# ConvGLU feed-forward of a hybrid decoder block: one 512-column product for both token parts

## The chip, the core and the metric

The kernel runs on one core of one Trainium2 chip. The metric is the device time of one launch in microseconds (us). TensorE (PE in the rows, PEld for its weight loads), VectorE (DVE), ScalarE (ACT), GpSimd (POOL) and the DMA queues work side by side and wait for one another by semaphores.

## The reference, cut to what matters

One decoder block on 256 tokens of width 1024: a mixing part with three branches (attention, a state-space scan, cross-attention to 256 memory tokens), merged and projected, and then a convolutional feed-forward part. The change works in the feed-forward part:

```python
def causal_dwconv(x, w, b):            # width 3, per channel
    ...
# in hybrid_layer:
    hid = causal_dwconv(rms_norm(h, ffn_norm_g) @ w_ffn_up, ffn_conv_w, ffn_conv_b)
    g_ff, up = jnp.split(hid, 2, axis=-1)
    return h + (jax.nn.silu(g_ff) * up) @ w_ffn_down
```

`w_ffn_up` is 1024 x 5632 (2816 gate columns and 2816 up columns), `w_ffn_down` is 2816 x 1024. All is float32.

## The kernel before

**Products in three parts.** A float32 operand is split into a high part that TensorE takes in one pass and a low part, the rest. Instead of a*b the kernel sums high*high, high*low and low*high (`three`, L364 to L366). Tokens stand as `tok_hi` and `tok_lo` (8 tiles of 128 x 256, features on partitions), weights as `w_hi` and `w_lo`.

**Weights** come in chunks of 128 x 2048 elements (1 MB) through three slots, 0 to 2. SyncE issues the load once the slot's raw tile has been used up (`lo_ready`), ScalarE makes `w_hi` by a copy (`split_hi`, L332, once TensorE has finished with the slot's last chunk: `gemm_done`), VectorE makes `w_lo` by a subtraction (`split_lo`, L336, `lo_ready`), and TensorE may then use the chunk. A slot thus holds one chunk at a time, and a round number `r` counts its chunks.

**The feed-forward part** has 11 steps (`F_STEPS`) of 256 hidden columns. Step f has a gate chunk (slot 0), an up chunk (slot 1) and a chunk of `w_ffn_down` (slot 2). TensorE's order is gate(f), up(f), down of step f - 1 (`ffn_step`); it is a hardware loop for f = 2 to 8, and the last two steps are written out. The gate chunk's result (two column tiles of 256 tokens) fills PSUM bank 0, the up chunk's bank 1; `down` adds into banks 4 to 7. At the end of the part come, in this order: gate(9), up(9), gate(10) from slot 2, up(10) from slot 0, down of step 8 from slot 1, down of step 9 from slot 2 and, in five pieces (`down_end`), down of step 10 from slot 0.

**VectorE's step** (`ffn` at L1698, `pad_with` at L1700) is a fixed order: `pad_g` = bank times the tokens' norm factor `rstd_b` (L1702), `split_lo` of the down chunk, four tap operations of the gate convolution (L1715), `pad_u` (L1702), `silu_g` (L1723), `split_lo` of the *next* step's gate chunk, four taps for up, `hid` (L1729), `split_lo` of the next up chunk, `hid_lo` (L1733). In the last step (10) the `split_lo` behind `silu_g` is that of the chunk for down of step 9.

**ScalarE's step** (`ffn` at L1238): it begins the gate convolution (L1246, two operations, waits for `pad_g` by `bank_free`), `split_hi` of the next gate chunk, `tanh_g` (L1253, waits for the taps), begins the up convolution (L1246), `split_hi` of the next up chunk, `hid_hi` (L1257), `split_hi` of the next down chunk.

Each engine does its instructions in the order written. TensorE's wait ahead of gate(f+1) is for `lo_ready[0]`, that is the `split_lo` behind `silu_g` in step f.

Of the kernel before, what the change touches and what calls it, by code (L numbers as in the profile page):

```python
# [104 lines left out]
def build(nc, x, mem, w_in, b_gate, w_mem_kv, w_br_attn, w_br_ssm, w_br_mem, w_out, w_ffn_up, w_ffn_down,  # L105
# [4 lines left out]
    def place(name, at, shape, dtype=F32):  # L110
        return nc.alloc_sbuf_tensor_at(name, [P, *shape], dtype, offset=base + int(at * KB))
# [5 lines left out]

    tok_hi = place("tok_hi", 72, [KT, T], F32R)
    tok_lo = place("tok_lo", 80, [KT, T], F32R)

# [231 lines left out]
    def cols_part(pe, s, j, ks, o, hi, lo, k0=0, start=True, stop=True, tiles=None, **kw):  # L352
# [99 lines left out]
    with nc.Block() as block:  # L452
# [128 lines left out]
        def _(pe):  # L581
# [311 lines left out]
            for s in (1, 2):  # L893
                pe.wait_ge(lo_ready[s], RF + 3)
                pe.wait_ge(bank_free[s], RF + 2)
                open_bank(pe, s)
                for j in range(2):
                    cols_part(pe, s, j, range(0, HK), ps[:, s, j * T:(j + 1) * T], tok_hi, tok_lo, start=False,
                              stop=False, skip_group_check=True)
                if s == 1:  # L900
                    pe.wait_ge(h_added, 3)
                    turn_h(2)
                    turn_h(3)
                    pe.wait_ge(h_rstd, NT)
# [3 lines left out]
                    mm.then_inc(h_spread, 1)  # L908
            pe.wait_ge(h_lo, KT)
# [13 lines left out]
            def ffn_step(f, first=False):  # L923
# [3 lines left out]
                down(r, 2, f, hid_hi, hid_lo, first)  # L927

            ffn_step(1, first=True)
            with pe.Fori(2, F_STEPS - 2) as f:  # L930
                ffn_step(f)
            gemm_cols(pe, RL - 1, 0, tok_hi, tok_lo)
            gemm_cols(pe, RL - 1, 1, tok_hi, tok_lo)
            pe.wait_ge(bank_free[2], RF + 3)
            gemm_cols(pe, RL - 1, 2, tok_hi, tok_lo, free=())
            gemm_cols(pe, RL, 0, tok_hi, tok_lo)
            down(RL, 1, F_STEPS - 2, hid_hi, hid_lo)
# [8 lines left out]
        def _(act):  # L946
# [320 lines left out]
            ffn(F_STEPS - 1, 2, RF + 4, 0, RL + 2, [(RL, 2)], [(RL + 1, 0)], [], hi=end_hi)  # L1267
            for n, (t, c0, width, _) in enumerate(Y_PARTS):
# [17 lines left out]
        def _(dve):  # L1286
# [193 lines left out]
            def heads(i, first=False):  # L1480
# [36 lines left out]
                if i == 1:  # L1517
                    dve.wait_ge(m_factor_in, 16)
# [178 lines left out]

            def ffn(f, sa, ra, sb, rb, early, after_gate, after_up, hi=hid_hi, lo=hid_lo):  # L1698
# [161 lines left out]
```

## Time and profile before

| | us |
|---|---|
| median of 3 runs | 684.38 (683.76 to 684.55) |
| the profiled execution | 683.92 |
| its span, first to last instruction | 682.1 |
| TensorE busy | 673.5 |
| VectorE busy | 493.5 |
| ScalarE busy | 371.5 |
| one feed-forward step, from one `pad_g` to the next | 16.98 |

Outside the span lie 683.92 - 682.1 = 1.8 us. A busy TensorE is not yet a TensorE at its peak: products overlap, so the distance from one start to the next is what one of them costs, and the duration shown (0.28 us for 256 columns) is how long it takes until its result is there. On the other engines, too, the next instruction may start a little before the one ahead is shown as ended.

### The profile page before, as it was taken

What the parts mean: (1) busy time and instruction counts of PE and PEld (TensorE: products, weight loads), DVE (VectorE), ACT (ScalarE), POOL (GpSimd) and SP (SyncE); (2) the same over time, 40 slices, a digit from 0 to 9 for tenths busy, and PEclk for the clock granted to TensorE, in tenths of its full rate; (3) what the DMA queues carried; (4) which work ended last, traced back from release to release, by engine and by line L of the source; (5) the groups of instructions that cost most, each with busy time, mean ns of one, the idle gap of its engine ahead of it and who ended that gap; (6) DMA issues with size and microseconds to landing.
All of it is one profiled execution on the core that took longest, in us unless ns stands there. A gap on an engine that the chain in (4) does not pass through costs nothing.

```text
span 682.1 us, 11417 instructions
## 1 busy us (share of the span) xinstructions
PE 673.5 (99%) x4505; PEld 616.4 (90%) x4505; DVE 493.5 (72%) x617; ACT 371.5 (54%) x462; POOL 10.4 (2%) x21
## 2 busy tenths in 40 slices
PE   8999999999999999999999999999999999999996
PEld 6999999999999989999888888888899999999995
DVE  6886979696866766777754655556688777777796
ACT  7568767767455544555533333443555555555552
POOL 0000000000100000000000000000100000000001
PEclk9999999999999999999999999999999999999999
DMA  9775868569185446545566655565445555555521
GB/s 297 240 256 181 247 198 263 164 217 326 62 270 171 145 163 232 180 140 171 178 211 218 214 194 182 195 231 173 166 140 191 188 185 190 180 189 183 193 87 62
DMA packets 99599, 130.92 MB, mean 192 GB/s; under 512 B 5615, under 2 KB 73708, under 8 KB 98924
## 3 DMA queue, kind: packets, MB, share of 16 engines
q1 hardware_dynamic: 98020, 125.27, 55.8%
q10 hardware_dynamic: 1544, 5.16, 2.3%
q8 instruction: 25, 0.41, 0.3%
q14 instruction: 10, 0.08, 0.0%
HBM read 129.31 MB, written 2.68 MB: 193 GB/s over the span
## 4 chain that ended last, share of the span: by engine, by line
PE 97%; DVE 1%; DMA 1%; ACT 0%; POOL 0%; issue 0%; POOLq 0%; SPq 0%; DVEq 0%; ACTq 0%
PE ps L364 31%; PE ps L365 30%; PE ps L366 30%; PE ps L678 1%; DMA x_nat<-x 1%; PE ps L679 1%; PE ps L419 1%; PE ps L663 1%; PE ps L698 1%; PE ps L715 1%; PE ps L706 0%; DVE h_nat L1750 0%; PE ps L697 0%; PE ps L717 0%; PE ps L771 0%; PE ps L666 0%
## 5 line engine op out<-in xcount | busy, mean ns | idle before, releaser
L336 DVE TENSOR_TENSOR w_lo<-w_raw,w_hi 128x2048 fp32r<-128x2048 f32 x107 | 244.6, 2287 | 88.0 <-ACT w_hi L332 88.0
L332 ACT ACTIVATE w_hi<-w_raw 128x2048 fp32r<-128x2048 f32 x107 | 204.3, 1911 | 99.1 <-PE ps L366 93.9
L364 PE MATMUL ps<-tok_hi,w_hi 128*128 128x256 f32 x864 | 246.6, 285 | 0.4 <-DVE tok_lo L1310 0.4
L365 PE MATMUL ps<-tok_lo,w_hi 128*128 128x256 f32 x864 | 244.4, 283 | 0.0
L366 PE MATMUL ps<-tok_hi,w_lo 128*128 128x256 f32 x864 | 244.4, 283 | 0.0
L364 PEld LDWEIGHTS ps<-tok_hi,w_hi 128*128 128x128 f32 x864 | 165.7, 192 | 2.0 <-issue 1.5
L365 PEld LDWEIGHTS ps<-tok_lo,w_hi 128*128 128x128 f32 x864 | 165.7, 192 | 0.4
L366 PEld LDWEIGHTS ps<-tok_hi,w_lo 128*128 128x128 f32 x864 | 165.7, 192 | 0.0
L364 PE MATMUL ps<-w_hi,tok_hi 128*128 128x512 f32 x128 | 50.2, 392 | 0.0
L365 PE MATMUL ps<-w_lo,tok_hi 128*128 128x512 f32 x128 | 49.9, 390 | 0.0
L366 PE MATMUL ps<-w_hi,tok_lo 128*128 128x512 f32 x128 | 49.8, 389 | 0.0
L1246 ACT ACTIVATE conv_g<-pad_g,params 128x256 f32<-128x256 f32 x22 | 12.1, 595 | 38.5 <-DVE pad_g L1702 38.5
L1395 DVE SCALAR_TENSOR_TENSOR conv_a<-pad_x,params,conv_a 128x256 f32<-128x256 f32 x72 | 29.5, 478 | 0.2
L366 PEld LDWEIGHTS ps<-w_hi,tok_lo 128*128 128x128 f32 x128 | 24.0, 188 | 5.1
L364 PEld LDWEIGHTS ps<-w_hi,tok_hi 128*128 128x128 f32 x128 | 24.1, 188 | 4.9 <-issue 0.2
L365 PEld LDWEIGHTS ps<-w_lo,tok_hi 128*128 128x128 f32 x128 | 24.0, 188 | 4.7
L364 PE MATMUL ps<-w_hi,hid_hi 128*128 128x512 f32 x72 | 28.1, 391 | 0.0
L365 PE MATMUL ps<-w_lo,hid_hi 128*128 128x512 f32 x72 | 28.1, 391 | 0.0
L366 PE MATMUL ps<-w_hi,hid_lo 128*128 128x512 f32 x72 | 28.0, 389 | 0.0
L364 PE MATMUL ps<-w_hi,os_hi 128*128 128x512 f32 x64 | 25.1, 392 | 0.0
L365 PE MATMUL ps<-w_lo,os_hi 128*128 128x512 f32 x64 | 24.9, 390 | 0.0
L366 PE MATMUL ps<-w_hi,os_lo 128*128 128x512 f32 x64 | 24.9, 389 | 0.0
(269 smaller groups left out, 1002.2 us busy)
## 6 DMA issues: line engine op xcount, KB each, us to landing
w_raw<-w_in SPq DMA_DIRECT2D x94, 512.0 KB, 4.8
w_raw<-w_ffn_up SPq DMA_DIRECT2D x44, 512.0 KB, 4.4
w_raw<-w_ffn_down SPq DMA_DIRECT2D x22, 512.0 KB, 4.1
w_raw<-w_mem_kv SPq DMA_DIRECT2D x16, 512.0 KB, 4.4
w_raw<-w_br_ssm SPq DMA_DIRECT2D x16, 512.0 KB, 4.9
acs_b<-acs_d ACTq DMA_DIRECT2D x4, 1024.0 KB, 6.3
w_raw<-w_br_attn SPq DMA_DIRECT2D x8, 512.0 KB, 4.8
w_raw<-w_br_mem SPq DMA_DIRECT2D x8, 512.0 KB, 4.6
```

The lines of the kernel that those rows point to most:

```text
L332: act.activation(w_hi[:, s, :], w_raw[:, s, :], ACT.Copy).then_inc(hi_ready[s], 1)
L336: dve.tensor_tensor(w_lo[:, s, :], w_raw[:, s, :], w_hi[:, s, :].bitcast(F32), ALU.subtract).then_inc(lo_ready[s], 1)
L364: pe.matmul(o, a[0], b[0], start=start, stop=False, **kw)
L365: pe.matmul(o, a[0], b[1], start=False, stop=False, **kw)
L366: return pe.matmul(o, a[1], b[0], start=False, stop=stop, **kw)
L419: return pe.transpose(ps[:, bank, o:o + P], src[:, t, k * P:(k + 1) * P], ident)
L663: mm = pe.transpose(ps[:, 3 + t, c * P:(c + 1) * P], conv_o[:, 2 + c, t * P:(t + 1) * P], ident)
L678: pe.matmul(o, x_dt[:, 0, h * SHD:(h + 1) * SHD], decay[:, h, 0:T], start=True, stop=False)
L679: mm = pe.matmul(o[:, P:T], x_dt[:, 1, h * SHD:(h + 1) * SHD], decay[:, h, T:T + P], start=False, stop=True)
L698: mm = pe.matmul(ps[:, 3 + a, P:3 * P], q_t[:, a, P:T], k_t[:, a, :], start=True, stop=True)
L1246: act.activation(conv[:, j, :], pad[:, j, FTAPS - 1:], ACT.Identity, bias=cols_up[:, FTAPS, bass.ds(c, 1)], scale=cols_up[:, FTAPS - 1, ba ...
L1395: dve.scalar_tensor_tensor(conv_a[:, s, j, :], pad_x[:, s, j, tap:tap + T], cols_conv[:, tap, bass.ds(conv_tile(s, j, g), 1)], conv_a[:, s ...
```

## The change

From step 2 on (`wide=True`) a gate or up chunk is multiplied otherwise. The two token parts now lie side by side in one tile `tok` (8 x 2 x 256), and one product of 512 columns of `w_hi` with both parts writes a whole PSUM bank: high*high in its left half, high*low in its right half. The third product (`w_lo` with the high part, 256 columns) adds to the left half. So a chunk's column tile fills a bank of its own, and a chunk fills two: banks 0 and 1 for gate, 2 and 3 for up. The sum of the halves is then made outside TensorE. ScalarE copies the right halves of both banks to `low_g` or `low_u`, VectorE adds the left halves to it (this frees the banks, `bank_free`), and multiplies by `rstd_b` in a second operation (`pad_scaled`). Steps 0 and 1, and all products ahead of the feed-forward part, are as they were. Some semaphores are merged: `m_factor_kept` and `m_factor_in` are one, and `h_spread` counts on `late_turned`, with the counts waited for set to match.

```diff
-    tok_hi = place("tok_hi", 72, [KT, T], F32R)
-    tok_lo = place("tok_lo", 80, [KT, T], F32R)
+    tok = place("tok", 72, [KT, 2, T], F32R)
+    tok_hi, tok_lo = tok[:, :, 0, :], tok[:, :, 1, :]
...
+    def gemm_both(pe, s, banks, both, other=None):
+        for j in range(2):
...
+            for k in range(KT):
+                w = slice(k * CW + j * P, k * CW + (j + 1) * P)
+                pe.matmul(ps[:, banks[j], :], w_hi[:, s, w], both[:, k], start=k == 0, stop=False)
+                mm = pe.matmul(ps[:, banks[j], 0:T], w_lo[:, s, w], both[:, k, 0, :], start=False, stop=k == KT - 1)
+        mm.then_inc(gemm_done[s], 1)
...
+            def wide_steps(r):
+                for s in range(2):
+                    pe.wait_ge(lo_ready[s], r + 2)
+                    pe.wait_ge(bank_free[s], r + 1)
+                    gemm_both(pe, s, F_BANKS[s], tok)
...
             with pe.Fori(2, F_STEPS - 2) as f:
-                ffn_step(f)
+                r = f + (RG - 1)
+                wide_steps(r)
+                down(r, 2, f, hid_hi, hid_lo)
+            wide_steps(RL - 1)
+            pe.wait_ge(lo_ready[2], RL + 1)
+            pe.wait_ge(bank_free[0], RL + 1)
+            gemm_both(pe, 2, F_BANKS[0], tok)
+            pe.wait_ge(lo_ready[0], RL + 2)
+            pe.wait_ge(bank_free[1], RL + 1)
+            gemm_both(pe, 0, F_BANKS[1], tok)
```

In ScalarE's `ffn`:

```diff
-                    act.wait_ge(bank_free[s], freed)
+                    if wide:
+                        act.wait_ge(gemm_done[s], freed - 1)
+                        act.activation(low[:], part_pair(F_BANKS[n], 1), ACT.Copy).then_inc(low_part, 1)
+                        act.wait_ge(pad_scaled, 2 * f + n - 3)
+                    else:
+                        act.wait_ge(bank_free[s], freed)
```

In VectorE's `pad_with`:

```diff
-                    dve.wait_ge(gemm_done[s], r + 1)
-                    dve.tensor_tensor(pad[:, :, FTAPS - 1:], halves(s), rstd_b[:].unsqueeze(1).to_broadcast([P, 2, T]),
-                                      ALU.mult).then_inc(bank_free[s], 1)
+                    if wide:
+                        n = int(pad is pad_u)
+                        dve.wait_ge(low_part, LOW0 + 2 * f + n - 3)
+                        dve.tensor_tensor(pad[:, :, FTAPS - 1:], part_pair(F_BANKS[n], 0), (low_g, low_u)[n][:],
+                                          ALU.add).then_inc(bank_free[s], 1)
+                        dve.wait_ge(bank_free[s], RF + 4 if s > 1 else r + 2)
+                        dve.tensor_tensor(pad[:, :, FTAPS - 1:], pad[:, :, FTAPS - 1:], rstd,
+                                          ALU.mult).then_inc(pad_scaled, 1)
```

ScalarE in step 9, the first that is written out (the loop's steps are in the same order). Before:

```order
L1246 ACTIVATE conv_g<-pad_g,params 128x256 [waits g_silu,bank_free0]
L1246 ACTIVATE conv_g<-pad_g,params 128x256
L332 ACTIVATE w_hi<-w_raw 128x2048 [waits gemm_done0,loaded0]
L1253 ACTIVATE tanh_g<-conv_g 128x512 [waits f_step]
L1246 ACTIVATE conv_u<-pad_u,params 128x256 [waits hid_done,bank_free1]
L1246 ACTIVATE conv_u<-pad_u,params 128x256
```

and now:

```order
L1277 ACTIVATE low_g<-ps 128x512 [waits gemm_done0]
L1285 ACTIVATE conv_g<-pad_g,params 128x256 [waits g_silu,pad_scaled]
L1285 ACTIVATE conv_g<-pad_g,params 128x256
L337 ACTIVATE w_hi<-w_raw 128x2048 [waits gemm_done0,loaded0]
L1292 ACTIVATE tanh_g<-conv_g 128x512 [waits f_step]
L1277 ACTIVATE low_u<-ps 128x512 [waits gemm_done1]
L1285 ACTIVATE conv_u<-pad_u,params 128x256 [waits hid_done,pad_scaled]
L1285 ACTIVATE conv_u<-pad_u,params 128x256
```

A copy out of PSUM stands ahead of each convolution's begin; that of the up chunk stands behind `tanh_g`, which waits for the taps (`f_step`).

VectorE in step 9 and, in its last rows, at the start of what follows. Before:

```order
L1702 TENSOR_TENSOR pad_g<-ps,rstd_b 128x2x256 [waits gemm_done0]
L336 TENSOR_TENSOR w_lo<-w_raw,w_hi 128x2048 [waits hi_ready2]
L1715 SCALAR_TENSOR_TENSOR conv_g<-pad_g,params,conv_g 128x256 [waits conv_begun] x2
L1715 SCALAR_TENSOR_TENSOR conv_g<-pad_g,params,conv_g 128x256 [waits f_step] x2
L1702 TENSOR_TENSOR pad_u<-ps,rstd_b 128x2x256 [waits gemm_done1]
L1723 SCALAR_TENSOR_TENSOR silu_g<-tanh_g,conv_g 128x512 [waits g_tanh]
L336 TENSOR_TENSOR w_lo<-w_raw,w_hi 128x2048 [waits hi_ready0]
```

and now:

```order
L1744 TENSOR_TENSOR pad_g<-ps,low_g 128x2x256 [waits low_part]
L1747 TENSOR_TENSOR pad_g<-pad_g,rstd_b 128x2x256 [waits bank_free0]
L341 TENSOR_TENSOR w_lo<-w_raw,w_hi 128x2048 [waits hi_ready2]
L1763 SCALAR_TENSOR_TENSOR conv_g<-pad_g,params,conv_g 128x256 [waits conv_begun] x2
L1763 SCALAR_TENSOR_TENSOR conv_g<-pad_g,params,conv_g 128x256 [waits f_step] x2
L1744 TENSOR_TENSOR pad_u<-ps,low_u 128x2x256 [waits low_part]
L1747 TENSOR_TENSOR pad_u<-pad_u,rstd_b 128x2x256 [waits bank_free1]
L1771 SCALAR_TENSOR_TENSOR silu_g<-tanh_g,conv_g 128x512 [waits g_tanh]
L341 TENSOR_TENSOR w_lo<-w_raw,w_hi 128x2048 [waits hi_ready0]
```

Each `pad_g` and `pad_u` is two operations, the first of which waits for ScalarE's copy (`low_part`) and no longer for TensorE; the last row is the `split_lo` of the chunk for up(10); in the loop it stands for the next step's gate chunk.

VectorE in step 10, from `last_lo` of step 9 to the `split_lo` of the chunk that down of step 9 uses (slot 2). Before:

```order
L1733 TENSOR_TENSOR last_lo<-hid,last_hi 128x512 [waits hid_hi_s]
L1702 TENSOR_TENSOR pad_g<-ps,rstd_b 128x2x256 [waits gemm_done2]
L1715 SCALAR_TENSOR_TENSOR conv_g<-pad_g,params,conv_g 128x256 [waits conv_begun] x2
L1715 SCALAR_TENSOR_TENSOR conv_g<-pad_g,params,conv_g 128x256 [waits f_step] x2
L1702 TENSOR_TENSOR pad_u<-ps,rstd_b 128x2x256 [waits gemm_done0]
L1723 SCALAR_TENSOR_TENSOR silu_g<-tanh_g,conv_g 128x512 [waits g_tanh]
L336 TENSOR_TENSOR w_lo<-w_raw,w_hi 128x2048 [waits hi_ready2]
```

and now:

```order
L1781 TENSOR_TENSOR last_lo<-hid,last_hi 128x512 [waits hid_hi_s]
L1744 TENSOR_TENSOR pad_g<-ps,low_g 128x2x256 [waits low_part]
L1747 TENSOR_TENSOR pad_g<-pad_g,rstd_b 128x2x256 [waits bank_free2]
L1763 SCALAR_TENSOR_TENSOR conv_g<-pad_g,params,conv_g 128x256 [waits conv_begun] x2
L1763 SCALAR_TENSOR_TENSOR conv_g<-pad_g,params,conv_g 128x256 [waits f_step] x2
L1744 TENSOR_TENSOR pad_u<-ps,low_u 128x2x256 [waits low_part]
L1747 TENSOR_TENSOR pad_u<-pad_u,rstd_b 128x2x256 [waits bank_free0]
L1771 SCALAR_TENSOR_TENSOR silu_g<-tanh_g,conv_g 128x512 [waits g_tanh]
L341 TENSOR_TENSOR w_lo<-w_raw,w_hi 128x2048 [waits hi_ready2]
```

Nothing of TensorE's work lies between these rows; both pads, the taps and `silu_g` stand ahead of that `split_lo`, and the pads are two operations each.

## Rows read from the trace of the kernel before

**Rows 1.** The page, part 1: busy time of each engine

```profile
PE 673.5 (99%) x4505; PEld 616.4 (90%) x4505; DVE 493.5 (72%) x617; ACT 371.5 (54%) x462; POOL 10.4 (2%) x21
```

**Rows 2.** The page, part 4: the chain that ended last, by engine

```profile
PE 97%; DVE 1%; DMA 1%; ACT 0%; POOL 0%; issue 0%; POOLq 0%; SPq 0%; DVEq 0%; ACTq 0%
```

**Rows 3.** Groups by line, 460 to 682 us: busy, mean ns | idle before, releaser

```profile
L1666 DVE TENSOR_TENSOR h_nat<-ps,h_nat 128x512 f32<-128x512 f32 x4 | 2.8, 689 | 3.2 <-PE ps L366 3.2
...
L1196 ACT ACTIVATE mg_hi<-ps 128x512 fp32r<-128x512 f32 x2 | 1.1, 596 | 3.9 <-PE ps L419 3.9
```

**Rows 4.** Timeline of TensorE, a loop step: start, us, what, [idle before]

```profile
562.85 0.40 PE L364 MATMUL ps<-w_hi,hid_hi 128*128 128x512 f32 x1
...
568.09 0.39 PE L366 MATMUL ps<-w_hi,hid_lo 128*128 128x512 f32 x1
568.32 0.28 PE L364 MATMUL ps<-tok_hi,w_hi 128*128 128x256 f32 x1
...
573.95 0.28 PE L366 MATMUL ps<-tok_hi,w_lo 128*128 128x256 f32 x1
```

**Rows 5.** Timeline of VectorE over one loop step

```profile
574.27 0.69 DVE L1702 TENSOR_TENSOR pad_g<-ps,rstd_b 128x512 f32<-128x512 f32 x1 [2.62 <-PE ps L366]
574.88 2.28 DVE L336 TENSOR_TENSOR w_lo<-w_raw,w_hi 128x2048 fp32r<-128x2048 f32 x1
577.08 1.66 DVE L1715 SCALAR_TENSOR_TENSOR conv_g<-pad_g,params,conv_g 128x256 f32<-128x256 f32 x4
580.03 0.69 DVE L1702 TENSOR_TENSOR pad_u<-ps,rstd_b 128x512 f32<-128x512 f32 x1 [1.29 <-PE ps L366]
580.64 0.68 DVE L1723 SCALAR_TENSOR_TENSOR silu_g<-tanh_g,conv_g 128x512 f32<-128x512 f32 x1
581.24 2.28 DVE L336 TENSOR_TENSOR w_lo<-w_raw,w_hi 128x2048 fp32r<-128x2048 f32 x1
583.44 1.66 DVE L1715 SCALAR_TENSOR_TENSOR conv_u<-pad_u,params,conv_u 128x256 f32<-128x256 f32 x4
...
591.25 0.69 DVE L1702 TENSOR_TENSOR pad_g<-ps,rstd_b 128x512 f32<-128x512 f32 x1 [2.62 <-PE ps L366]
```

**Rows 6.** Timeline of ScalarE in the same step

```profile
575.20 1.10 ACT L1246 ACTIVATE conv_g<-pad_g,params 128x256 f32<-128x256 f32 x2 [3.88 <-DVE pad_g L1702]
...
578.78 0.63 ACT L1253 ACTIVATE tanh_g<-conv_g 128x512 f32<-128x512 f32 x1 [0.67 <-DVE conv_g L1715]
...
585.87 0.63 ACT L1257 ACTIVATE hid_hi<-hid 128x512 fp32r<-128x512 f32 x1 [2.06 <-DVE hid L1729]
586.40 1.90 ACT L332 ACTIVATE w_hi<-w_raw 128x2048 fp32r<-128x2048 f32 x1
```

**Rows 7.** Timeline of VectorE, steps 9 (first row) and 10

```profile
642.19 0.69 DVE L1702 TENSOR_TENSOR pad_g<-ps,rstd_b 128x512 f32<-128x512 f32 x1 [2.62 <-PE ps L366]
...
656.55 0.68 DVE L1702 TENSOR_TENSOR pad_g<-ps,rstd_b 128x512 f32<-128x512 f32 x1
657.90 1.77 DVE L1715 SCALAR_TENSOR_TENSOR conv_g<-pad_g,params,conv_g 128x256 f32<-128x256 f32 x4 [0.67 <-ACT conv_g L1246]
...
661.32 2.29 DVE L336 TENSOR_TENSOR w_lo<-w_raw,w_hi 128x2048 fp32r<-128x2048 f32 x1
```

**Rows 8.** Timeline of ScalarE, step 10: `tanh_g`

```profile
660.07 0.61 ACT L1253 ACTIVATE tanh_g<-conv_g 128x512 f32<-128x512 f32 x1
```

**Rows 9.** Timeline of TensorE, the first product of down of step 9

```profile
664.74 0.39 PE L364 MATMUL ps<-w_hi,last_hi 128*128 128x512 f32 x1
```

**Rows 10.** Timeline of VectorE, then TensorE, near 9 us: a start after a wait

```profile
9.06 0.48 DVE L1310 SCALAR_TENSOR_TENSOR tok_lo<-ps,cols_mix,tok_hi 128x256 fp32r<-128x256 f32 x1 [0.48 <-ACT tok_hi L964]
...
9.70 0.35 PE L364 MATMUL ps<-tok_hi,w_hi 128*128 128x256 f32 x1 [0.45 <-DVE tok_lo L1310]
9.89 0.28 PE L365 MATMUL ps<-tok_lo,w_hi 128*128 128x256 f32 x1
```

**Rows 11.** Timeline of TensorE, its first products, before anything else runs

```profile
0.98 4.59 PE L413 MATMUL ps<-zero_s 128*128 128x512 bf16 x13 [0.98 <-DVE zero_s L1287]
```

More of the change, by code:

```diff
@@ L60 @@
 SLOTS = 3
+LOW0 = 0
 Q = 32
@@ L65 @@
 HK = KT // 2
+F_BANKS = (0, 1), (2, 3)
 V_BANKS, G1_BANKS, OUT_BANKS, H_BANKS = (2, 5), (0, 7), ((2, 3), (6, 7)), (4, 5, 0, 3)
@@ L225, in build @@
     silu_g = place("silu_g", R + 10.5, [2, T])
+    low_g = place("low_g", R + 24, [2, T])
+    low_u = place("low_u", R + 26, [2, T])
     hid = place("hid", R + 12.5, [2, T])
@@ L360, in cols_part @@
         return mm
+    def gemm_both(pe, s, banks, both, other=None):
+        for j in range(2):
+            if other is not None and j:
+                pe.wait_ge(*other)
+            for k in range(KT):
[3 more added lines that the diff above has]
+        mm.then_inc(gemm_done[s], 1)
     def three(pe, o, a, b, start, stop, **kw):
@@ L927, in ffn_step @@
                 down(r, 2, f, hid_hi, hid_lo, first)
+            def wide_steps(r):
[3 more added lines that the diff above has]
+                    gemm_both(pe, s, F_BANKS[s], tok)
             ffn_step(1, first=True)
+            pe.wait_ge(bank_free[1], RG + 2)
+            pe.wait_ge(bank_free[2], RF + 3)
             with pe.Fori(2, F_STEPS - 2) as f:
-                ffn_step(f)
[L932 to L936, printed above, removed]
+                r = f + (RG - 1)
[8 more added lines that the diff above has]
+            gemm_both(pe, 0, F_BANKS[1], tok)
             down(RL, 1, F_STEPS - 2, hid_hi, hid_lo)
@@ L1235, in _, with ffn @@
             split_hi(act, RG, 0)
-            def ffn(f, sa, na, sb, nb, after_gate, after_up, last, first=False, hi=hid_hi):
-                for n, (s, freed, pad, conv, tile) in enumerate(((sa, na, pad_g, conv_g, 0),
-                                                                 (sb, nb, pad_u, conv_u, FT))):
-                    act.wait_ge(bank_free[s], freed)
+            def ffn(f, sa, na, sb, nb, after_gate, after_up, last, first=False, hi=hid_hi, wide=True):
+                for n, (s, freed, pad, conv, tile, low) in enumerate(((sa, na, pad_g, conv_g, 0, low_g),
+                                                                      (sb, nb, pad_u, conv_u, FT, low_u))):
+                    if wide:
[4 more added lines that the diff above has]
+                        act.wait_ge(bank_free[s], freed)
                     if not first:
@@ L1259, in ffn @@
                     split_hi(act, rr, ss)
-            ffn(0, 1, RF + 3, 2, RF + 3, [(RG, 1)], [(RG, 2)], [(RG + 1, 0)], first=True)
-            ffn(1, 0, RG + 2, 1, RG + 2, [], [(RG + 1, 1)], [(RG + 1, 2)])
+            ffn(0, 1, RF + 3, 2, RF + 3, [(RG, 1)], [(RG, 2)], [(RG + 1, 0)], first=True, wide=False)
+            ffn(1, 0, RG + 2, 1, RG + 2, [], [(RG + 1, 1)], [(RG + 1, 2)], wide=False)
             with act.Fori(2, F_STEPS - 2) as f:
@@ L1695, in _, with ffn @@
             dve.wait_ge(pads_zero, 2)
-            def ffn(f, sa, ra, sb, rb, early, after_gate, after_up, hi=hid_hi, lo=hid_lo):
+            def ffn(f, sa, ra, sb, rb, early, after_gate, after_up, hi=hid_hi, lo=hid_lo, wide=True):
                 def pad_with(s, r, pad, splits):
-                    dve.wait_ge(gemm_done[s], r + 1)
-                    dve.tensor_tensor(pad[:, :, FTAPS - 1:], halves(s), rstd_b[:].unsqueeze(1).to_broadcast([P, 2, T]),
-                                      ALU.mult).then_inc(bank_free[s], 1)
+                    rstd = rstd_b[:].unsqueeze(1).to_broadcast([P, 2, T])
+                    if wide:
[6 more added lines that the diff above has]
+                                          ALU.mult).then_inc(pad_scaled, 1)
+                    else:
+                        dve.wait_ge(gemm_done[s], r + 1)
+                        dve.tensor_tensor(pad[:, :, FTAPS - 1:], halves(s), rstd, ALU.mult).then_inc(bank_free[s], 1)
                     for rr, ss in splits:
```

29 lines of the change are left out of this document (16 added, 13 removed).

## The prediction, made before the kernel had run

> **What bounds the kernel now.** I read the page's first part and its chain first. TensorE is busy for 673.5 of 682.1 us [rows 1], and the chain that ended last is 97% TensorE [rows 2]. So the time is that of TensorE's stream, and only two things count: how many microseconds of products the change takes out, and whether the stream begins to wait. For the second I read the timelines of one step. The step is 591.25 - 574.27 = 16.98 us [rows 5]. VectorE waits in it twice for TensorE, 2.62 us ahead of `pad_g` and 1.29 us ahead of `pad_u` [rows 5]: 3.91 us of slack in all. That is what the change spends from.
>
> **What TensorE saves.** What a product costs is the distance between starts. 24 products of 512 columns stand from 562.85 to 568.32, 0.228 each (0.227 without the first), and 48 of 256 columns from 568.32 on, the last at 573.95: 5.63 / 47 = 0.120 [rows 4]. Before, a pair high*high and high*low with its third product costs 3 x 0.120 = 0.360; now 0.227 + 0.120 = 0.347. A chunk has 16 such sets: 5.76 us before, 5.55 now. Nine steps have 18 chunks: 288 x 0.013 = 3.7 us is the most that can be won, and one step of TensorE becomes 2 x 5.55 + 24 x 0.227 = 16.55 us. The product count falls by a third and the gain is small, since columns are what costs: 512 and 256 columns at 2.4 GHz take 0.213 and 0.107, so each product has 0.013 to 0.014 us beside its columns.
>
> The Trainium skill, "TensorE: Matmul & The Clock Gate", section "Back-to-back issue gap", gives N / 2.4 + 2.5 ns. The trace does not agree, with 13 ns. By the page's figure a chunk would be (estimate) 16 x 0.0025 = 0.04 us shorter instead of 0.21, and the sum below some 1.4 us higher.
>
> **What VectorE and ScalarE get.** VectorE gets one operation of 512 elements more for each pad: `pad_g` takes 0.69 and the next starts 0.61 after it [rows 5]. An add of PSUM and an SBUF tile takes the same 0.689 [rows 3]. But the multiply waits for the add by a semaphore, so it starts at its end: 0.69 + 0.03 = 0.72 (0.61 is the lower bound). ScalarE gets a copy of 512 elements out of PSUM, 0.596 by `mg_hi` [rows 3]; the nearest from SBUF, `hid_hi`, is 0.63 [rows 6]. In sums of busy time it all fits (VectorE 16.98 - 3.91 + 2 x 0.72 = 14.5 of 16.55). It is the order that matters. `low_u` stands behind `tanh_g`, and `tanh_g` waits for VectorE's taps; so VectorE stands still from the taps' end until `tanh_g` and the copy are through, and behind the stopped `pad_u` are queued `silu_g` and the `split_lo` that TensorE's next gate chunk waits for.
>
> **The chain of a loop step**, from the end of gate(f)'s last product as zero (before: 573.95 + 0.28 = 574.24, and `pad_g` started 0.03 later [rows 4, 5]). Estimates, each from a row:
> - `low_g` 0.03 to 0.63; add 0.66; multiply 1.38; `split_lo` of the down chunk 0.61 later, 1.99; taps 2.20 later (577.08 - 574.88), 4.19, done 1.66 later, 5.85 [rows 5];
> - `tanh_g` 0.04 later (578.78 against 577.08 + 1.66), 5.89; `low_u` 0.54 behind it (as `w_hi` behind `hid_hi`, 586.40 - 585.87) [rows 6], 6.43 to 7.03;
> - add 7.06, multiply 7.78, `silu_g` 8.39, `split_lo` of the next gate chunk 8.99, done 2.28 later: 11.27.
>
> Before, the same chain without the copies and adds, less the 1.29 us that it waited for up(f), ended about 3.3 us earlier, and TensorE never felt it. TensorE itself wants gate(f+1) when up and down are through: its next start is 0.12 - 0.28 = -0.17, plus 5.55 + 5.45 = 10.83. So it now waits, where it did not before. A start after a wait costs more: `tok_lo` ends at 9.06 + 0.48 = 9.54, the product starts at 9.70 (0.15 later with unrounded times) and the next one 0.19 instead of 0.12 behind it [rows 10]. I add 0.05 for a register instruction that stands between the wait and the product in the loop. Gate(f+1) thus ends at 11.27 + 0.15 + 0.07 + 0.05 + 5.43 (to the start of its last product: 16 x 0.227 + 15 x 0.120) + 0.28 = 17.25. **That is the new step: 17.25 us against 16.98**, with TensorE idle for some 0.6 to 0.7 us in each.
>
> Other chains of the step are shorter. VectorE's: from the up taps to the next `pad_g` it has 591.25 - 583.44 - 2.62 = 5.19 us of work [rows 5]; the taps now begin at 8.99 + 2.20 = 11.19, so it is free at 16.4. ScalarE's: `hid` is done about 13.6, `hid_hi` and `split_hi` take 0.54 + 1.9, so it is free at 16.1. Both are ahead of 17.25. Loads are asked for by the `split_lo` that empties a slot and have about a step's time; they do not come up.
>
> **The end.** From gate(9)'s end as zero (before: 642.19 - 0.03 = 642.16 [rows 7]). Up to the next chunk's `split_lo` (for up(10)) it is the same chain, so down of step 8 ends at 22.5, as before (664.74 - 642.16 = 22.58 [rows 9]): what the shorter chunks give back the wait takes. But VectorE goes into step 10 late. It has `last_lo` at 15.70 and no idle time from there: add 16.31, multiply 17.03. Before, the taps began 1.35 behind the pad (657.90 - 656.55 [rows 7]), now 18.38; `tanh_g` 2.17 behind their begin (660.07 [rows 8]), 20.55; `low_u` 0.51 later, 21.06 to 21.66; add 21.69, multiply 22.41, `silu_g` 23.02, `split_lo` of the chunk for down of step 9 23.63 to 25.92. Before it was done at 661.32 + 2.29 - 642.16 = 21.45 [rows 7], 1.1 us before TensorE wanted it. Now TensorE stands from 22.5 to 25.92 + 0.22 = 26.14: **3.6 us**. Behind it nothing waits more: `end_lo` ends at 31.0, down of step 9 at 31.6.
>
> **The sum** against the profiled execution, 683.92: gate(2) ends 16 x 0.013 = 0.2 earlier; seven steps from gate(2) to gate(9) at +0.27 are +1.9; the end +3.6. 683.92 - 0.2 + 1.9 + 3.6 = **689.2 us**. The profiled execution is 0.5 under the median of 684.38, so I give 689.4.
>
> Bounds of this case: with the multiply at 0.61 behind the add and no register term, a step is 0.27 shorter, which makes the loop +0.0, and the end +3.3: 687. With waits that cost 0.24 as ahead of `conv_g` (574.27 + 0.69 = 574.96, and it starts at 575.20 [rows 5, 6]) instead of 0.03 at three places of the chain, a step is 0.6 longer: +4.4 in the loop and 0.6 at the end, 694.
>
> **Rivals.**
> 1. *TensorE stays the bound everywhere*, because the chain of copies and adds is at least 0.6 us shorter per step than I make it and step 10 catches up. For: sums of busy time leave VectorE 2 us. Against: the order. It gives 683.92 - 3.7 = 680.3 (faster).
> 2. *The loop fits, the end does not*: the chain is some 0.6 us shorter, the last `split_lo` late all the same. -0.2 - 7 x 0.43 + 3.6: 684.3 (no change).
> 3. *Handoffs dearer* than 0.03, the bound above: 694 (slower).
> 4. *TensorE's clock falls in the stop of 3.6 us at the end*, longer than any idle time of TensorE in this trace, and its last products run at half rate for a while. TensorE's first 13 products of 512 columns, which follow idle time, take 4.59 us [rows 11], so (4.59 - 0.38) / 12 = 0.35 from start to start against 0.227 later: 1.5 us for such a spell. It gives 691. The Trainium skill, same page, Part 1, says that the clock gate halves the clock again after idle time; whether a stop of this length does it no row here shows.
>
> **How the numbers follow.** My forecast 0.70 (687 to 694), rival 1 0.07, rival 2 0.09, rival 3 0.07, rival 4 0.07. A difference of 0.2% (1.4 us) is about what a measurement of this kernel can tell from no change. Faster 0.07. Same 0.10, rival 2 and a little of the forecast's low end. Slower 0.83. The range takes in rival 2 and the upper bound: 684 to 694.5.
>
> **What would show it.** Right: TensorE idle 0.5 to 0.8 us in each of the loop's steps, the releaser `w_lo` of VectorE; a step of 17.1 to 17.4; `pad_g` and `pad_u` released by ScalarE's copies; one idle time of TensorE of 3 to 4 us behind down of step 8. Pitches of 0.227 and 0.120 in turn. Wrong: no idle time of TensorE (rival 1), steps of 16.6 with a late end (rival 2), over 17.6 (rival 3), pitches of about twice these behind the stop (rival 4).

## The result

| | us |
|---|---|
| before, median of 5 runs | 684.25 (683.76 to 684.55) |
| changed kernel, median of 5 runs | 692.25 (690.81 to 692.77) |
| ratio | 1.0112, 95% interval 1.0101 to 1.0124 |
| profiled execution before / now | 683.92 / 691.45 |
| its span before / now | 682.1 / 689.6 |

The changed kernel is slower by 8.0 us. The prediction was 689.4 us, slower, with 684.0 to 694.5 as its range: the sign and the range held, the time was 2.9 us too low.

The page of the changed kernel, parts 1 and 4, against [rows 1] and [rows 2]:

```profile
PE 675.5 (98%) x4217; PEld 601.4 (87%) x4217; DVE 506.1 (73%) x635; ACT 381.2 (55%) x480; POOL 10.5 (2%) x21
...
PE 74%; DVE 14%; ACT 5%; issue 4%; DMA 1%; DVEq 0%; ACTq 0%; POOL 0%; POOLq 0%
```

There are 288 products fewer, and the chain that ended last, 97% TensorE before, now runs for a fifth of the time over VectorE and ScalarE. Busy shares hardly moved. The waits of TensorE in the changed kernel (who waited for whom: us in total, times, longest) say where they stand between:

```profile
PE ps L381 <- DVE w_lo L341: 3.5, 1, 3.5
PE ps L375 <- DVE w_lo L341: 2.4, 7, 0.4
```

Seven waits for the split of a gate chunk, of steps 3 to 9 (L375 is the 512-column product), and one long one at the end. Idle time on TensorE's row is less than it lost, since the last product's shown duration covers a part of each wait. So I read the step itself. VectorE over the same loop step as in [rows 5]:

```profile
576.06 0.69 DVE L1744 TENSOR_TENSOR pad_g<-ps,low_g 128x512 f32<-128x512 f32 x1 [1.60 <-ACT low_g L1277]
576.78 0.69 DVE L1747 TENSOR_TENSOR pad_g<-pad_g,rstd_b 128x512 f32<-128x512 f32 x1
577.39 2.28 DVE L341 TENSOR_TENSOR w_lo<-w_raw,w_hi 128x2048 fp32r<-128x2048 f32 x1
579.60 1.67 DVE L1763 SCALAR_TENSOR_TENSOR conv_g<-pad_g,params,conv_g 128x256 f32<-128x256 f32 x4
582.45 0.69 DVE L1744 TENSOR_TENSOR pad_u<-ps,low_u 128x512 f32<-128x512 f32 x1 [1.18 <-ACT low_u L1277]
583.17 0.69 DVE L1747 TENSOR_TENSOR pad_u<-pad_u,rstd_b 128x512 f32<-128x512 f32 x1
583.78 0.68 DVE L1771 SCALAR_TENSOR_TENSOR silu_g<-tanh_g,conv_g 128x512 f32<-128x512 f32 x1
584.38 2.29 DVE L341 TENSOR_TENSOR w_lo<-w_raw,w_hi 128x2048 fp32r<-128x2048 f32 x1
...
593.28 0.69 DVE L1744 TENSOR_TENSOR pad_g<-ps,low_g 128x512 f32<-128x512 f32 x1 [1.50 <-ACT low_g L1277]
```

The step is 593.28 - 576.06 = 17.22 us against 16.98. VectorE stands still for 1.18 us ahead of `pad_u`, and it is no longer TensorE that ends this but ScalarE's copy. ScalarE in this stretch, and TensorE at the start of the next gate chunk:

```profile
575.43 0.60 ACT L1277 ACTIVATE low_g<-ps 128x512 f32<-128x512 f32 x1 [1.30 <-PE ps L376]
...
581.30 0.63 ACT L1292 ACTIVATE tanh_g<-conv_g 128x512 f32<-128x512 f32 x1 [0.74 <-DVE conv_g L1763]
581.84 0.58 ACT L1277 ACTIVATE low_u<-ps 128x512 f32<-128x512 f32 x1
```

```profile
586.11 0.39 PE L383 MATMUL ps<-w_hi,hid_lo 128*128 128x512 f32 x1
586.80 0.49 PE L375 MATMUL ps<-tok,w_hi 128*128 128x512 f32 x1 [0.30 <-DVE w_lo L341]
587.13 0.27 PE L376 MATMUL ps<-tok,w_lo 128*128 128x256 f32 x1
587.25 0.40 PE L375 MATMUL ps<-tok,w_hi 128*128 128x512 f32 x1
```

From 586.11 the next start would have been due 0.23 later, at 586.34; it came at 586.80, 0.13 behind the split's end (584.38 + 2.29 = 586.67), and its successor 0.33 behind it. That is 0.46 of standing and 0.10 of slow restart in this step. All the loop's steps are 17.22 to 17.32 us long.

The end of the feed-forward part, TensorE from the last product of down of step 8 on (against [rows 9], where there is no gap):

```profile
666.64 0.39 PE L383 MATMUL ps<-w_hi,hid_lo 128*128 128x512 f32 x1
670.53 0.47 PE L381 MATMUL ps<-w_hi,last_hi 128*128 128x512 f32 x1 [3.51 <-DVE w_lo L341]
670.84 0.40 PE L382 MATMUL ps<-w_lo,last_hi 128*128 128x512 f32 x1
671.07 0.43 PE L383 MATMUL ps<-w_hi,last_lo 128*128 128x512 f32 x1
671.31 0.62 PE L381 MATMUL ps<-w_hi,last_hi 128*128 128x512 f32 x1
671.72 0.63 PE L382 MATMUL ps<-w_lo,last_hi 128*128 128x512 f32 x1
...
674.28 0.59 PE L382 MATMUL ps<-w_lo,last_hi 128*128 128x512 f32 x1
674.71 0.40 PE L383 MATMUL ps<-w_hi,last_lo 128*128 128x512 f32 x1
674.95 0.39 PE L381 MATMUL ps<-w_hi,last_hi 128*128 128x512 f32 x1
```

Behind the stop of 3.89 us from start to start (0.23 is due, so TensorE stands for 3.66) the first three products still go at the old pace. Only then, 0.8 us after the work has begun again, do they stand 0.41 to 0.43 apart, for some 3.4 us, and then 0.23 again. The clock granted in these stretches (the columns are the stretch; its length, then PE, PEld, DVE, ACT and POOL busy; PEclk, DMA share, GB/s):

```profile
671.30:674.70 3.40, 3.40 (x9) 2.64 (x8) 3.29 (x4) 0.63 (x1) 0.00 (x0) 0.50 0.00 0
674.80:677.90 3.10, 3.10 (x15) 2.55 (x14) 0.77 (x2) 0.00 (x0) 0.00 (x0) 1.00 0.03 5
```

0.50 is the lower of the two levels, 1.2 GHz.

**The account of the two profiled executions**, start to end:

| stretch | before | now | difference |
|---|---|---|---|
| first instruction to `pad_g` of step 0 | 497.81 | 498.24 | +0.43 |
| to the end of gate(2) | 25.49 | 25.38 | -0.11 |
| gate(2) to gate(9), seven steps | 118.86 | 120.80 | +1.94 |
| end of gate(9) to the first product of down of step 9 | 22.58 | 26.11 | +3.53 |
| from there to the last instruction's end | 17.39 | 19.12 | +1.73 |

The sum is 7.52 us. The first row is not the change's doing. ScalarE waits 4.1 us for a transfer (`acs_b`) and goes on at 49.33, before 2.6 us and at 48.05; near 82 us TensorE then stands 0.4 us for VectorE's `conv_o`, which it did not before. In two variants below (only the end in the new form, and the copy moved), whose code up to there is that of the changed kernel, the transfer is awaited until 48.6, this wait is missing, and `pad_g` starts at 497.73 and 497.58. The clock also rose later at the very start of this execution, but that is made up by 10 us, where TensorE is 0.1 to 0.2 us ahead of the execution before.

### The profile page after: what moved, and what is told of

It reads as the page before. It is cut to its first block, busy times and chain, and to the rows that moved or that the text cites. A ratio compares the mean times of both kernels' runs of the same rounds, so it can differ in the third digit from the quotient of the medians.

```text
span 689.6 us, 10899 instructions
## 1 busy us (share of the span) xinstructions
PE 675.5 (98%) x4217; PEld 601.4 (87%) x4217; DVE 506.1 (73%) x635; ACT 381.2 (55%) x480; POOL 10.5 (2%) x21
## 4 chain that ended last, share of the span: by engine, by line
PE 74%; DVE 14%; ACT 5%; issue 4%; DMA 1%; DVEq 0%; ACTq 0%; POOL 0%; POOLq 0%
PE ps L381 20%; PE ps L382 20%; PE ps L383 20%; DVE w_lo L341 5%; PE ps L375 5%; PE ps L376 2%; DVE conv_a L1434 2%; DVE conv_g L1763 1%; DMA acs_b<-acs_d 1%; DVE pad_u L1744 1%; DVE pad_g L1747 1%; DVE pad_g L1744 1%; DVE silu_g L1771 1%; PE ps L699 1%; ACT conv_g L1285 1%
## 5 line engine op out<-in xcount | busy, mean ns | idle before, releaser
L381 PE MATMUL ps<-tok,w_hi 128*128 128x256 f32 x576 | 165.2, 287 | 0.4 <-DVE tok L1349 0.4
L382 PE MATMUL ps<-tok,w_hi 128*128 128x256 f32 x576 | 162.9, 283 | 0.0
L383 PE MATMUL ps<-tok,w_lo 128*128 128x256 f32 x576 | 162.9, 283 | 0.0
L381 PEld LDWEIGHTS ps<-tok,w_hi 128*128 128x128 f32 x576 | 110.4, 192 | 1.6 <-issue 1.5
L382 PEld LDWEIGHTS ps<-tok,w_hi 128*128 128x128 f32 x576 | 110.4, 192 | 0.1
L383 PEld LDWEIGHTS ps<-tok,w_lo 128*128 128x128 f32 x576 | 110.4, 192 | 0.0
L375 PE MATMUL ps<-tok,w_hi 128*128 128x512 f32 x288 | 102.0, 399 | 2.4 <-DVE w_lo L341 2.4
L376 PE MATMUL ps<-tok,w_lo 128*128 128x256 f32 x288 | 80.4, 279 | 0.0
L375 PEld LDWEIGHTS ps<-tok,w_hi 128*128 128x128 f32 x288 | 54.0, 188 | 18.2 <-issue 4.7
L376 PEld LDWEIGHTS ps<-tok,w_lo 128*128 128x128 f32 x288 | 54.3, 188 | 0.0
L381 PE MATMUL ps<-w_hi,tok 128*128 128x512 f32 x128 | 50.2, 392 | 0.0
L382 PE MATMUL ps<-w_lo,tok 128*128 128x512 f32 x128 | 49.9, 390 | 0.0
L383 PE MATMUL ps<-w_hi,tok 128*128 128x512 f32 x128 | 49.8, 389 | 0.0
L383 PEld LDWEIGHTS ps<-w_hi,tok 128*128 128x128 f32 x128 | 24.0, 188 | 5.1
L381 PEld LDWEIGHTS ps<-w_hi,tok 128*128 128x128 f32 x128 | 24.0, 188 | 4.9 <-issue 0.2
L382 PEld LDWEIGHTS ps<-w_lo,tok 128*128 128x128 f32 x128 | 24.1, 188 | 4.8
```

The costliest lines, as they stand in the source:

```text
L375: pe.matmul(ps[:, banks[j], :], w_hi[:, s, w], both[:, k], start=k == 0, stop=False)
L376: mm = pe.matmul(ps[:, banks[j], 0:T], w_lo[:, s, w], both[:, k, 0, :], start=False, stop=k == KT - 1)
```

## Experiments

Theory: the time is set by a chain of waits in the order of the instructions, not by any engine's load, and the end pays a second time, for the stop and for the clock behind it. The rivals are named with each run.

### One half of the change at a time

Steps 9 and 10 back to the old form:

```diff
-            wide_steps(RL - 1)
...
+            gemm_cols(pe, RL - 1, 0, tok_hi, tok_lo)
+            gemm_cols(pe, RL - 1, 1, tok_hi, tok_lo)
+            gemm_cols(pe, RL - 1, 2, tok_hi, tok_lo, free=())
+            gemm_cols(pe, RL, 0, tok_hi, tok_lo)
...
-            ffn(F_STEPS - 1, 2, RL + 1, 0, RL + 2, [(RL, 2)], [(RL + 1, 0)], [], hi=end_hi)
+            ffn(F_STEPS - 1, 2, RF + 4, 0, RL + 2, [(RL, 2)], [(RL + 1, 0)], [], hi=end_hi, wide=False)
```

> Steps 9 and 10 back to three products of 256 columns, one pad operation and no copy; steps 2 to 8 as in the changed kernel. Theory (the chain copy, add, multiply, taps, tanh, copy, add, multiply, silu, split ahead of the next gate chunk sets the loop step; the end has a cost of its own because VectorE enters step 10 late): loop steps of 17.25 us, no idle time of TensorE behind down of step 8, TensorE's clock at its upper level to the end; 684.25 + 1.9 = 686.2 us. Rival (the two products of different width themselves cost more, wherever they stand): 14 of 18 chunks remain, so most of the 8 us remains, about 690.

Measured: 686.38 us (8 runs, 685.49 to 686.89), before beside it 684.06; ratio 1.0029, interval 1.0019 to 1.0040. Loop steps are 17.22 to 17.33, and between gate(9) and down of step 9 lie 22.6 us again, with TensorE in one stream from gate(9) on.

The other half, the loop as before and steps 9 and 10 in the new form (ScalarE's and VectorE's loops take the old form too, and the counts waited for are set to match, not shown):

```diff
             with pe.Fori(2, F_STEPS - 2) as f:
-                r = f + (RG - 1)
-                wide_steps(r)
-                down(r, 2, f, hid_hi, hid_lo)
+                ffn_step(f)
```

> The other half: steps 2 to 8 as before, only steps 9 and 10 with the 512-column products, the copies and two pad operations. Theory: loop steps of 16.98, the stop of 3.6 to 3.9 us behind down of step 8 is there, and behind it TensorE's products at 0.427 from start to start for some 3.4 us (1.7 us lost): 684.25 - 0.2 + 3.6 + 1.7 = 689.4 us. Rival (the stop comes from the delay that has been gathered over the loop): no stop, 684 us.

Measured: 689.74 us (4 runs), before 684.06; ratio 1.0076, interval 1.0059 to 1.0092. All loop steps are 16.98. TensorE's timeline has the stop, and below it stands the granted clock of the stretch behind (0.50):

```profile
668.08 0.76 PE L381 MATMUL ps<-w_hi,last_hi 128*128 128x512 f32 x1 [3.41 <-DVE w_lo L341]
668.64 0.63 PE L382 MATMUL ps<-w_lo,last_hi 128*128 128x512 f32 x1
```

```profile
666.80:673.50 6.70, 5.42 (x13) 4.28 (x14) 6.21 (x8) 1.89 (x2) 0.00 (x0) 0.50 0.00 0
```

So the stop does not come from a delay gathered in the loop; two steps are enough. The halves cost 2.3 and 5.7 us, together 8.0, the whole change 8.0: they add up, and over two thirds of the loss is in two steps of nine.

One thing was not as expected. In the profiled execution of the second half the clock fell earlier, within the stop, and stayed low for 6.8 us and not 3.4; from the first product of down of step 9 to the end it takes 20.1 us, 2.7 more than before and not 1.7. So what the clock costs behind one and the same stop differs from one execution to another.

### Order or load

The same work on each engine, with ScalarE's copy of the up chunk moved ahead of `tanh_g`:

```diff
                     if wide:
-                        act.wait_ge(gemm_done[s], freed - 1)
-                        act.activation(low[:], part_pair(F_BANKS[n], 1), ACT.Copy).then_inc(low_part, 1)
+                        if n == 0:
+                            act.wait_ge(gemm_done[s], freed - 1)
+                            act.activation(low[:], part_pair(F_BANKS[n], 1), ACT.Copy).then_inc(low_part, 1)
...
                     if n == 0:
+                        if wide:
+                            act.wait_ge(gemm_done[sb], nb - 1)
+                            act.activation(low_u[:], part_pair(F_BANKS[1], 1), ACT.Copy).then_inc(low_part, 1)
                         act.wait_ge(f_step, 8 * f + 4)
                         act.activation(tanh_g[:], conv_g[:], ACT.Tanh).then_inc(g_tanh, 1)
```

> Changed kernel, but ScalarE copies the up chunk's right halves ahead of tanh_g instead of behind it; the same work on every engine. Theory (order, not load): the copy then starts when up(f) ends, 5.57 us behind the gate chunk's end instead of 6.43, the next split of the gate chunk is done at 10.4 instead of 11.3, before TensorE wants it (10.8): loop steps of 16.55, TensorE without idle time in the loop. At the end the stop behind down of step 8 shrinks to about 2.9 us. Sum 684.25 - 3.2 + 2.2 = 683.3 us, 685 if TensorE's clock falls all the same. Rival (VectorE's two more operations a step are what costs): steps stay at 17.2 and the time at 692.

Measured: 686.50 us (9 runs, 684.67 to 687.70), before 684.06; ratio 1.0032, interval 1.0022 to 1.0042. The timelines of ScalarE and of VectorE in its profiled execution (684.67 us):

```profile
579.02 0.60 ACT L1294 ACTIVATE low_u<-ps 128x512 f32<-128x512 f32 x1 [0.52 <-PE ps L376]
579.51 0.62 ACT L1296 ACTIVATE tanh_g<-conv_g 128x512 f32<-128x512 f32 x1
```

```profile
579.65 0.69 DVE L1748 TENSOR_TENSOR pad_u<-ps,low_u 128x512 f32<-128x512 f32 x1 [0.45 <-ACT low_u L1294]
```

`pad_u` waits 0.45 us instead of 1.18, TensorE has no wait left in the loop, and all loop steps are 16.79 us, down from 17.22 to 17.32. The order was the bound, and VectorE's load was not. But 16.79 is not the 16.55 that I had worked out for TensorE alone. The stop at the end shrinks to 2.83 us from start to start, that is 2.60 of standing (expected 2.9), and in this execution the clock stays up behind it. The runs spread over 3.0 us, before over 1.0. Four of the six highest have a mean granted clock of 0.994 to 0.996 over their span, the profiled one 0.998 and every run of the kernel before 0.997 to 0.999: it looks as if the clock fell in some of them behind the stop. They have no profile, and this mean also counts the idle time at the end of a run, so this is argued. The median is 3.2 us over the 683.3 that I had expected, of which the missing 0.24 us a step is 1.7.

The opposite test adds work of one size at two places. A second copy of 512 elements, to an unused tile, once between `tanh_g` and `low_u` (from PSUM):

```diff
+                        if n == 1:
+                            act.activation(twice[:], part_pair(F_BANKS[n], 1), ACT.Copy)
                         act.activation(low[:], part_pair(F_BANKS[n], 1), ACT.Copy).then_inc(low_part, 1)
```

> Changed kernel with a second copy of the up chunk's right halves to an unused tile, between tanh_g and the copy that counts, so on the chain. Theory: each loop step 0.54 longer (17.8), seven of them 3.8, and 1.1 at the end: 692.25 + 4.9 = 697.1 us. Rival (ScalarE has slack, 45% idle, so a copy costs nothing wherever it stands): 692.2.

Measured: 696.38 us (4 runs), ratio to before 1.0177, interval 1.0161 to 1.0193. Loop steps of 17.71 (one of 17.81): 0.48 longer each, as the copies stand 0.48 apart:

```profile
584.25 0.63 ACT L1295 ACTIVATE tanh_g<-conv_g 128x512 f32<-128x512 f32 x1 [0.74 <-DVE conv_g L1766]
584.78 0.58 ACT L1279 ACTIVATE twice<-ps 128x512 f32<-128x512 f32 x1
585.26 0.59 ACT L1280 ACTIVATE low_u<-ps 128x512 f32<-128x512 f32 x1
```

And once behind `hid_hi` (from `hid`, in SBUF):

```diff
                 act.activation(hi[:], hid[:], ACT.Copy).then_inc(hid_hi_s, 1)
+                if wide:
+                    act.activation(twice[:], hid[:], ACT.Copy)
```

> Changed kernel with the same kind of copy (512 elements, to an unused tile) behind hid_hi, off the chain. Theory: ScalarE is free at 16.7 of 17.25 all the same, so nothing changes: 692.2 us, steps of 17.25. Rival (any work on ScalarE or its writes cost): up to 697.

Measured: 692.10 us (4 runs), ratio 1.0120, interval 1.0105 to 1.0136, steps of 17.22 to 17.32: nothing. A copy of the same size on the same engine costs 4 us at one place and nothing at the other. The one reads PSUM and the other SBUF, but the step grew by just the 0.48 for which the first holds up `low_u`.

Taking away from the chain, the multiply by the norm factor left out (ScalarE waits for the add instead):

```diff
-                        dve.wait_ge(bank_free[s], RF + 4 if s > 1 else r + 2)
-                        dve.tensor_tensor(pad[:, :, FTAPS - 1:], pad[:, :, FTAPS - 1:], rstd,
-                                          ALU.mult).then_inc(pad_scaled, 1)
```

> Changed kernel without the multiply by the norm factor in steps 2 to 10 (this part of the computation is left out). Theory: the chain is 2 x 0.72 shorter (15.8 us), so TensorE sets the step, 16.55; at the end the stop is 1.3 us instead of 3.6 and the clock stays up: 684.25 - 3.2 + 0.7 = 681.8 us. Rival (the copy and the wait for another engine are the cost, not the second operation): steps of 17, 688.

Measured: 683.56 us (10 runs), ratio 0.9991, interval 0.9981 to 1.0000, 1.8 us over my number. Its steps are 16.79 as well, and the stop at the end is 1.17 us from start to start, 0.94 of standing (expected 1.3). `pad_u` still waits 1.19 us for the copy, so ScalarE's copy and its wait alone would not have made the change lose. What I missed is the same 0.24 us a step as above.

### The clock behind the stop

Twelve products of zeros, into a bank that is free by then, between down of step 8 and down of step 9:

```diff
+            pe.wait_ge(bank_free[2], RF + 4)
+            z = zero_s[:].bitcast(mybir.dt.bfloat16)
+            for _ in range(12):
+                pe.matmul(ps[:, 0, :].rearrange("p (a n) -> p a n", n=P), z, z.unsqueeze(1).to_broadcast([P, 4, P]),
+                          start=True, stop=True)
             down(RL, 2, F_STEPS - 1, last_hi, last_lo)
```

> Changed kernel with 12 products of zeros (512 columns, into bank 0, which is free by then) between down of step 8 and down of step 9, that is within TensorE's stop, about 2.6 us of them. Theory (the stop lets the clock fall, and the products behind it run at half rate for 3.4 us): the granted clock stays at its upper level, starts at 0.227, and the time falls by 1.7 us to 690.5. Rival (the slow products come from something else, as from the operands or the bank): no change, 692.2, or slower by the zeros' own time.

Measured: 690.31 us (4 runs, 690.12 to 690.48), 1.9 under the changed kernel; ratio to before 1.0088, interval 1.0071 to 1.0105. TensorE's timeline, and below it the stretch behind the stop (granted clock 1.00):

```profile
667.28 2.76 PE L975 MATMUL ps<-zero_s 128*128 128x512 bf16 x12
670.84 0.47 PE L381 MATMUL ps<-w_hi,last_hi 128*128 128x512 f32 x1 [0.80 <-DVE w_lo L341]
671.15 0.39 PE L382 MATMUL ps<-w_lo,last_hi 128*128 128x512 f32 x1
671.38 0.39 PE L383 MATMUL ps<-w_hi,last_lo 128*128 128x512 f32 x1
```

```profile
670.90:676.30 5.40, 5.40 (x24) 4.50 (x25) 4.88 (x7) 0.63 (x1) 0.00 (x0) 1.00 0.01 3
```

The first product of down of step 9 starts no earlier against the end of gate(9) (26.1 us in both), the granted clock stays at 1.00 and the starts at 0.23. So it was the idle time that let the clock fall, and the slow products were its cost.

### A version with both faults out, and the missing 0.24 us

The copy ahead of `tanh_g` in the loop and the old form in steps 9 and 10, that is both edits above:

> ScalarE's copy of the up chunk ahead of tanh_g in steps 2 to 8, steps 9 and 10 as before the change. Theory: loop steps of 16.55, nothing late at the end: 14 chunks x 0.21 = 2.9 us less than before, 681.3 us, faster than both kernels. Rival (load of VectorE): 17.2 a step, 686.

Measured: 682.73 us (11 runs), before 684.09; ratio 0.9981, interval 0.9972 to 0.9990. It beats both kernels, but by 1.4 us instead of 2.9. Its steps are 16.79 with TensorE in one stream:

```profile
570.28 0.40 PE L375 MATMUL ps<-tok,w_hi 128*128 128x512 f32 x1
570.52 0.28 PE L376 MATMUL ps<-tok,w_lo 128*128 128x256 f32 x1
570.64 0.40 PE L375 MATMUL ps<-tok,w_hi 128*128 128x512 f32 x1
```

From each 512-column product to the 256-column one behind it is 0.236 (the median), and from that to the next 0.117. A set costs 0.353 and not 0.347, and the change saves 0.007 a set and not 0.013. Over the 32 sets of a step that is 0.2 of the missing 0.24 us. Whether the turn from one width to the other does that or the operands themselves was open, so the same products in another order:

```diff
             for k in range(KT):
                 w = slice(k * CW + j * P, k * CW + (j + 1) * P)
                 pe.matmul(ps[:, banks[j], :], w_hi[:, s, w], both[:, k], start=k == 0, stop=False)
+            for k in range(KT):
+                w = slice(k * CW + j * P, k * CW + (j + 1) * P)
                 mm = pe.matmul(ps[:, banks[j], 0:T], w_lo[:, s, w], both[:, k, 0, :], start=False, stop=k == KT - 1)
```

> As e5_low_first_tail_narrow (copy ahead of tanh_g, steps 9 and 10 as before the change), but in each column tile first the eight products of 512 columns and then the eight of 256, instead of in turn; the same products. Theory A (the step is 16.79 instead of 16.55 us because a 512-column product followed by one of 256 columns takes 0.236 instead of 0.227: it is the turn from one width to the other): eight sets take 8 x 0.227 + 8 x 0.120 = 2.78 instead of 2.82 us, a loop step 16.6, 14 chunks 1.2 us less, 681.5 us. Theory B (a 512-column product of these operands, from the double token tile into a whole bank, takes 0.236 wherever it stands): 0.236 between them here too, and no change or somewhat more, 682.7 to 683.3 us.

Measured: 681.71 us (6 runs), before 683.91; ratio 0.9967, interval 0.9954 to 0.9979, the fastest of all. Its steps are 16.61. TensorE, one column tile:

```profile
584.51 1.98 PE L375 MATMUL ps<-tok,w_hi 128*128 128x512 f32 x8
586.32 1.11 PE L378 MATMUL ps<-tok,w_lo 128*128 128x256 f32 x8
587.27 2.00 PE L375 MATMUL ps<-tok,w_hi 128*128 128x512 f32 x8
```

(586.32 - 584.51) / 8 = 0.226 and (587.27 - 586.32) / 8 = 0.119, 0.345 a set: the operands take what any product of their width takes, and grouping gives the missing time back. But the turn from one width to the other is not enough for it. TensorE in the changed kernel, the second and the last 512-column product of the gate chunk of two neighbouring steps, 5 and 6:

```profile
569.93 0.40 PE L375 MATMUL ps<-tok,w_hi 128*128 128x512 f32 x1
...
575.23 0.40 PE L375 MATMUL ps<-tok,w_hi 128*128 128x512 f32 x1
```

```profile
587.25 0.40 PE L375 MATMUL ps<-tok,w_hi 128*128 128x512 f32 x1
...
592.45 0.39 PE L375 MATMUL ps<-tok,w_hi 128*128 128x512 f32 x1
```

The order of widths is the same in both, with 15 sets between: 0.353 a set in the first and 0.347 in the second. Behind their short stops four of the six loop steps 3 to 8 run at 0.347 and two, 5 and 8, at 0.353; those two are the steps of 17.32 us. Where TensorE does not stop in the loop (the version with both edits, the moved copy, the kernel without the multiply) each step is at 0.353. What picks one pitch or the other is open.

## Why the prediction was right, and where not

**The chain of a loop step** was right item by item. With the end of gate(f) at 575.43 - 0.03 = 575.40 the rows give: add 0.66 (forecast 0.66), multiply 1.38 (1.38), split 1.99 (1.99), taps 4.20 (4.19), `tanh_g` 5.90 (5.89), `low_u` 6.44 (6.43), add 7.05 (7.06), multiply 7.77 (7.78), `silu_g` 8.38 (8.39), split 8.98 to 11.27 (8.99 to 11.27), step 17.22 (17.25). Seven steps cost 1.94 us (forecast 1.9). That the multiply starts 0.72 behind the add for its wait, and 0.61 is what an operation without one takes, stands in the rows too: 576.78 - 576.06, and 577.39 - 576.78.

**The rest of the step's sum** was close too. I had put in 0.15 and 0.05 more for a register instruction, a term that no run shows (the product starts 0.13 behind the split), and 0.07 for the slow restart (0.10 measured); the gate chunk's sets stand 0.347 apart in this step, as forecast. That is the 0.03 between 17.25 and 17.22. That "0.227 + 0.120 = 0.347" held here was partly luck: each pitch was read within a stretch of one width, the new code alternates, and in two of the six steps a set took 0.353, which makes them 17.32. Where TensorE is the bound every set does: 16.79 against 16.55, and three expectations built on the term (moved copy, left out multiply, the version with both edits) were too low, by 3.2, 1.8 and 1.4 us.

**The end** was right in place and size: down of step 9 starts 26.11 us behind gate(9), forecast 26.14; the stop was charged 3.6 and cost 3.53 (TensorE stands for 3.66 against 3.6).

**The clock was the miss.** I kept it as a rival with a chance of 0.07 and 1.5 us, beside the forecast, and it came together with the forecast: 1.73 us in the account, 1.9 by the run with zeros. The step that failed is the chance, not the mechanism: the price read from [rows 11] was near for this execution (the one with only the end in the new form paid 2.7), but a stop longer than any in the trace of before deserved more than 0.07, since no row spoke against it. The Trainium skill's rule that the gate halves the clock after idle time ("TensorE: Matmul & The Clock Gate", Part 1) agrees with the stop of 3.9 us here. With the 1.7 us for the clock the forecast would have been 691.1.

**The rest** of the 2.9 us is 0.43 ahead of the changed code in the profiled execution, 0.1 from smaller terms, and 0.6 by which the median lies further above the profiled execution (0.8) than I had allowed. That allowance was 0.2, though the sentence on it names 0.5. Longer spells of the low clock in other executions may be behind the 0.6; no profile shows it.

**The rivals** on the other side are out: TensorE did not stay the bound (the sum there, 683.92 - 3.7, is 680.2 and not 680.3), and dearer handoffs did not show (0.03 to 0.04 between engines; the one of 0.2 ahead of `conv_g` is off the chain). The Trainium skill's 2.5 ns beside a product's columns ("Back-to-back issue gap" of the same page, where it is the figure for isolated products) does not fit either order here: 13 ns in a stretch of one width, and 353 - 320 = 33 ns for the two of a set in turn where it takes 0.353.

## What to carry to other kernels

Where TensorE runs without a gap and a change sends its result through other engines, follow it to the next thing that TensorE waits for, in the order of the instructions, and add up each handoff; sums of busy time allowed this change (VectorE 14.5 of 16.6 us) and it lost all the same. A copy on a half idle engine is free or costs its full time depending on the instruction it stands behind, so place it behind the event that it needs, not behind one that comes later. Price a stop of TensorE together with the clock behind it, and where a gain hangs on some ns a product, read their cost in the order of widths, and with the stops, with which they will run.

## What the runs showed of the hardware that was not expected

- Products of 512 and 256 columns in turn take one of two pitches at the same granted clock of 1.00: 0.353 us a pair (a median of 0.236 and 0.117) in each loop step without a stop, and behind a short stop 0.347 in four steps and 0.353 in two (the changed kernel). In groups of eight of a width a pair takes 0.345 (1.81 + 0.95 us for eight).
- TensorE's granted clock fell to the lower level at each profiled stop of 3.8 to 4.3 us from start to start (the changed kernel, the one with the new form in steps 9 and 10 alone, the two with an added copy), and stayed up at stops of 2.8 and 1.2 us and at one that was filled with products of zeros up to its last 1.2 us.
- It fell at different moments: in the changed kernel 0.8 us after the products had begun again, in the one with the new form in steps 9 and 10 alone 2.4 us after the last product ahead of the stop had started. It stayed low for 3.4 us in the first (1.7 us lost) and for 6.8 in the second (2.7 lost).
- After a stop the first product keeps its successor waiting: 0.31 to 0.33 instead of 0.23 to 0.24 from start to start for 512 columns.
- The copy of 512 elements out of PSUM took ScalarE 0.58 behind `tanh_g` and 0.60 behind a wait.
